# Transposing the hidden activations of the expert blocks on TensorE instead of VectorE

## The reference

```
def expert_block(args):                      # xb: rows of one expert, e: which one
    xb, e = args
    hb = jax.nn.silu(xb @ w_gate[e]) * (xb @ w_up[e])
    return hb @ w_down[e]

y = lax.map(expert_block, (buf.reshape(n_blocks, MOE_BLOCK, D), block_e)).reshape(n_blocks * MOE_BLOCK, D)
out = jnp.zeros((N, D), x.dtype).at[tok_sorted].add(y[dest] * w_sorted[:, None])
```

## Time and profile before

| | |
|---|---|
| median of 3 executions | 3587.28 us (3582.31 to 3591.69) |
| the profiled execution | 3582.31 us, its span 3580.3 us |
| mean granted TensorE clock in it | 0.934 of full speed |
| busy over the span | TensorE 3176.8 us (89%), VectorE 1404.8 (39%), ScalarE 673.8 (19%) |
| first expert stage | 408.31 to 714.46 us |
| second expert stage | 1163.58 to 1472.36 us |

### The profile page before, as it was taken

One profiled execution on the slowest core, in us unless ns is written; L12 is line 12 of the kernel. 1 busy time (PEld: TensorE's weight loads), 2 busy tenths in 40 slices (PEclk: granted clock), 3 DMA queues, 4 the chain that ended last, 5 costly groups with the idle time before them and its releaser, 6 DMA issues. The chain is left out here.

```text
span 3580.3 us, 42191 instructions
## 1 busy us (share of the span) xinstructions
PE 3176.8 (89%) x15899; PEld 1565.7 (44%) x15899; DVE 1404.8 (39%) x3366; ACT 673.8 (19%) x1430; POOL 341.1 (10%) x434
## 2 busy tenths in 40 slices
PE   8889698859967988479999999898699999999998
PEld 5455333324544333244444444664443443444344
DVE  6533333333352333408999920563322122212222
ACT  1143122132221222210110110452110101001011
POOL 0023011110202111100000000123000000000000
PEclk9999799969988999789999999999799999999999
DMA  7861799831013999443335345755399999999994
GB/s 261 230 251 66 260 372 366 307 110 45 12 60 111 356 364 361 176 171 113 121 119 130 115 147 177 299 194 206 116 396 406 422 406 405 404 423 406 405 410 203
DMA packets 282431, 886.16 MB, mean 248 GB/s; under 512 B 35704, under 2 KB 75520, under 8 KB 233168
## 3 DMA queue, kind: packets, MB, share of 16 engines
q1 hardware_dynamic: 254032, 806.79, 60.3%
q0 software_dynamic: 28288, 77.91, 6.1%
HBM read 803.59 MB, written 80.99 MB: 247 GB/s over the span
## 5 line engine op out<-in xcount | busy, mean ns | idle before, releaser
L3047 PE MATMUL ec_gu<-ec_ring,ec_xg 128*64 128x512 f32 x2048 | 454.6, 595 | 0.9 <-ACT ec_xg L3199 0.9
L245 PE MATMUL proj_ps<-xT,proj_w 128*128 128x512 f32 x992 | 431.9, 597 | 0.9 <-DMA proj_w<-in_na_w_in 0.9
L245 PE MATMUL proj_ps<-proj_w,xT 128*128 128x512 f32 (+2 forms) x896 | 358.4, 562 | 22.2 <-DMA proj_w<-in_w_in 22.2
L245 PEld LDWEIGHTS proj_ps<-xT,proj_w 128*128 128x128 f32 x992 | 189.7, 192 | 239.3 <-issue 237.7
L3047 PEld LDWEIGHTS ec_gu<-ec_ring,ec_xg 128*64 128x64 f32 x2048 | 142.0, 137 | 303.3 <-issue 303.3
L245 PEld LDWEIGHTS proj_ps<-proj_w,xT 128*128 128x128 f32 x896 | 171.4, 192 | 207.4 <-issue 154.6
L3076 PE MATMUL ec_yp<-ec_ring,ec_hT 128*64 128x512 f32 x1024 | 248.2, 635 | 0.0
L1350 PE MATMUL moe_gu_ps<-moe_w,moe_xg 128*64 128x512 f32 x1024 | 231.4, 605 | 17.6 <-DMA moe_w<-in_exp_w_up 11.3
L274 ACT ACTIVATE proj_o<-proj_ps 128x512 f32<-128x512 f32 (+1 forms) x120 | 70.8, 590 | 611.4 <-PE proj_ps L245 611.4
L1413 DVE TENSOR_TENSOR moe_sig<-moe_sig,moe_gu_ps 64x512 f32<-64x512 f32 x32 | 21.7, 679 | 395.3 <-ACT moe_up L1457 395.3
L2225 DVE SCALAR_TENSOR_TENSOR band_big<-proj_hit,proj_row,band_big 128x516 f32<-128x516 f32 x256 | 173.5, 751 | 2.4
(11 more groups left out here) (515 smaller groups left out, 3871.0 us busy)
## 6 DMA issues: line engine op xcount, KB each, us to landing
ec_ring<-in_w_gate SPq DMA_DIRECT2D x128, 1024.0 KB, 9.6
ec_ring<-in_w_up SPq DMA_DIRECT2D x128, 1024.0 KB, 11.7
ec_ring<-in_w_down SPq DMA_DIRECT2D x128, 1024.0 KB, 12.3
moe_w<-in_exp_w_gate SPq DMA_DIRECT2D x32, 2048.0 KB
moe_w<-in_exp_w_up SPq DMA_DIRECT2D x32, 2048.0 KB
moe_w<-in_exp_w_down SPq DMA_DIRECT2D x32, 2048.0 KB, 21.0
proj_w<-in_w_in SPq DMA_DIRECT2D x22, 2048.0 KB, 11.0
proj_w<-in_w_ada SPq DMA_DIRECT2D x16, 1536.0 KB
```

The costliest lines, as they stand in the source:

```text
L245: mm = nc.tensor.matmul(bank[0:jb["op"], 0:jb["ow"]], lhs, rhs, start=(k == 0), stop=(k == nk - 1))
L3047: mm = nc.tensor.matmul(gu_ps[n][half, :], xg[:, k, c0:c0 + CAP], w[:, m * D_FF + n * 512:m * D_FF + (n + 1) * 512], start=(k == 0), stop= ...
```

## The change

The hidden values are no longer turned by VectorE. After gate/up of both blocks TensorE multiplies each 64x128 piece of hid and thid with the identity (`turn_h`), into a PSUM bank h_ps, and VectorE copies the bank to hT with two instructions a block (`turn`). The bank is the second of the two that x had: x now has one bank for both halves (the very first half excepted, which uses h_ps before it is needed), so the second half of x is turned only after ScalarE has copied the first, and the order of the three engines is rewritten around that. hT_main and hT_tail become one counter, hT_ready, counted when a block's hT is complete.

```diff
-        x_ps = [st.ps(f"x_ps{h}") for h in range(2)]
+        x_ps, h_ps = st.ps("x_ps"), st.ps("h_ps")
...
                 def turn_x(b, r, i, h):
                     if h == 0:
                         pe.wait_ge(xs_ready[r], 16 * i + 16)
-                    pe.wait_ge(xg_copied, 2 * b + h - 1)
+                    pe.wait_ge(xg_copied, 2 * b + h + 1)
                     for c in range(4):
-                        mm = nc.tensor.transpose(x_ps[h][:, c * MB:(c + 1) * MB], xs[r][:, (4 * h + c) * P:(4 * h + c + 1) * P],
+                        mm = nc.tensor.transpose(x_ps[:, c * MB:(c + 1) * MB], xs[r][:, (4 * h + c) * P:(4 * h + c + 1) * P],
                                                  ident[0:MB, 0:MB])
                     mm.then_inc(turned, 1)
...
+                def turn_h(i, r):
+                    b = 2 * i + r
+                    pe.wait_ge(hid_main, b + 3)
+                    pe.wait_ge(hT_ready, b + 1)
+                    for f in range(KF):
+                        nc.tensor.matmul(h_ps[:, f * MAIN:(f + 1) * MAIN], hid[r][:, f * P:(f + 1) * P],
+                                         ident[0:MAIN, 0:MAIN], start=True, stop=True)
+                    pe.wait_ge(hid_tail, b + 3)
+                    for c in range(2):
+                        c0 = (KF + c) * MAIN
+                        mm = nc.tensor.matmul(h_ps[:, c0:c0 + MAIN], thid[r][:, c * P:(c + 1) * P], ident[0:MAIN, 0:MAIN],
+                                              start=True, stop=True)
+                    mm.then_inc(hT_ps_ready, 1)
+
                 def down(i, r):
                     b = 2 * i + r
-                    pe.wait_ge(hT_main, b + 1)
+                    pe.wait_ge(hT_ready, b + 2)
...
-                    pe.wait_ge(hT_tail, b + 1)
...
                 def body(i, more):
                     gate_up(i, 0)
                     turn_x(2 * i + 1, 1, i, 0)
+                    gate_up_tail(i, 0)
                     turn_x(2 * i + 1, 1, i, 1)
-                    gate_up_tail(i, 0)
                     gate_up(i, 1)
                     gate_up_tail(i, 1)
+                    turn_h(i, 0)
                     if more:
                         turn_x(2 * i + 2, 0, i, 0)
+                    down(i, 0)
+                    if more:
                         turn_x(2 * i + 2, 0, i, 1)
-                    down(i, 0)
+                    turn_h(i, 1)
                     down(i, 1)
...
-                    V.drain()
-                    for fq in range(P // QD):
-                        for tb in range(MAIN // QD):
-                            e = V.transpose(hT[r][fq * QD:(fq + 1) * QD, :, tb * QD:(tb + 1) * QD],
-                                            by_f(hid[r][tb * QD:(tb + 1) * QD, :])[:, :, fq * QD:(fq + 1) * QD])
-                    e.then_inc(hT_main, 1)
...
+                def turn(i, r):
+                    dve.wait_ge(hT_ps_ready, 2 * i + r + 1)
+                    V.tensor_copy(hT[r][:, :, 0:MAIN], h_ps[:, 0:KF * MAIN].rearrange("p (f s) -> p f s", s=MAIN))
+                    V.tensor_copy(hT[r][:, :, MAIN:MB].rearrange("p (h c) s -> p h c s", c=2),
+                                  h_ps[:, KF * MAIN:(KF + 2) * MAIN].rearrange("p (c h s) -> p h c s", c=2, h=2))
+                    V.drain().then_inc(hT_ready, 1)
+
                 def body(i):
                     hidden(i, 0)
                     hidden(i, 1)
+                    turn(i, 0)
+                    turn(i, 1)
...
                 def body(i, more):
                     main(i, 0)
                     copy_x(2 * i + 1, 1, 0)
+                    tail(i, 0)
                     copy_x(2 * i + 1, 1, 1)
-                    tail(i, 0)
                     main(i, 1)
                     tail(i, 1)
                     if more:
                         copy_x(2 * i + 2, 0, 0)
+                    rows_out(i, 0)
+                    if more:
                         copy_x(2 * i + 2, 0, 1)
-                    rows_out(i, 0)
                     rows_out(i, 1)
```

More of the change, by code:

```diff
@@ L1255, in moe_experts @@
     MB, MAIN, TAIL = MOE_ROWS, 64, 32
-    QD = 32
     lo, hi = slice(0, MAIN), slice(MAIN, P)
@@ L1275, in moe_experts @@
         hid_main, hid_tail = st.sem("hid_main"), st.sem("hid_tail")
-        hT_main, hT_tail = st.sem("hT_main"), st.sem("hT_tail")
+        hT_ps_ready, hT_ready = st.sem("hT_ps_ready"), st.sem("hT_ready")
         down_ready, y_copied = st.sem("down_ready"), st.sem("y_copied")
@@ L1324, in first_x @@
                 def first_x(h):
-                    bank = x_ps[h]
+                    bank = (x_ps, h_ps)[h]
                     for c in range(4):
@@ L1343, in gate_up @@
                     b = 2 * i + r
-                    pe.wait_ge(xg_copied, 2 * b + 2)
+                    pe.wait_ge(xg_copied, 2 * b + 3)
                     for n in range(2):
@@ L1406, in _ @@
                 dve.sem_inc(hid_tail, 2)
+                dve.sem_inc(hT_ready, 1)
                 n1 = pairs_less_one(dve)
-                by_f = lambda v: v.rearrange("p (f q) -> p f q", q=P)
                 def hidden(i, r):
@@ L1441, in _ @@
             def _(act):
+                act.sem_inc(xg_copied, 1)
                 act.sem_inc(turned, 1)
@@ L1447, in _, with copy_x @@
                 n1 = pairs_less_one(act)
-                def copy_x(b, r, h):
+                def copy_x(b, r, h, bank=x_ps):
                     act.wait_ge(turned, 2 * b + h + 2)
-                    nc.scalar.activation(xg[r][:, 4 * h:4 * h + 4, :].rearrange("p c s -> p (c s)"), x_ps[h][:, 0:4 * MB],
+                    nc.scalar.activation(xg[r][:, 4 * h:4 * h + 4, :].rearrange("p c s -> p (c s)"), bank[:, 0:4 * MB],
                                          ACT.Copy).then_inc(xg_copied, 1)
@@ L1480, in body @@
                         copy_x(2 * i + 2, 0, 0)
+                    rows_out(i, 0)
+                    if more:
                         copy_x(2 * i + 2, 0, 1)
-                    rows_out(i, 0)
                     rows_out(i, 1)
                 copy_x(0, 0, 0)
-                copy_x(0, 0, 1)
+                copy_x(0, 0, 1, h_ps)
                 with act.Fori(0, n1) as i:
```

## The result

The changed kernel takes 3623.02 us, the median of four executions (3619.35 to 3626.52), against 3589.14 for the kernel before, also four (3582.31 to 3591.69). The ratio is 1.0101, with a 95% interval of 1.0082 to 1.0121: the change costs about 1%. The forecast was 3618 in a range of 3598 to 3656. The execution profiled was the highest of its four, 3626.52 us (span 3624.6), and the one profiled before was the lowest of its four; the spans differ by 44.3 us, the medians by 33.9. Three more executions of the changed kernel are on record, at 3618.15, 3626.57 and 3634.03 us.

A forecast was written before the change was run, and what follows sets the result against it. DMA transfers were taken to set the expert stages' pace, TensorE having 3.1 to 3.9 us slack a pair. Layers added 18.3 + 14.6 = 32.9 us to the profiled 3582.31, giving 3615.2; forecast 3618, half way towards the median's base, range 3598 to 3656.

The forecast's parts named there:

- Wait A: Before gate/up of block 1: TensorE waits for ScalarE to copy x after block 0's tail; 1.1 us added a pair.
- Wait B: Before the first down: VectorE copies block 0's turned hidden values only after block 1's products; 1.9 us added a pair.
- Wait C: Between the two downs: turning block 1's hidden values, then waiting for VectorE's copies; 1.7 us added a pair.
- The chain: TensorE's path through one steady pair of blocks: 34.96 us without DMA wait, plus 4.7, makes 39.66 us.
- The turns: TensorE's 12 matmul records turning one block's hidden values: 0.12 us each, 1.4 us; rival at ec_h's 3.0 us, chance 0.12.
- The bound moves from DMA to TensorE: Steady pairs: 39.66 us on TensorE exceeds the transfers' 38.06 and 38.87, so only the part above the slack is paid.
- The rival "faster": Steady pairs: DMA waits come of queue order, so pairs follow TensorE's path; with 2 us added, 3575 us; chance 0.05.
- The clock: Rival at the downs: small work and waits drop TensorE to 1.2 GHz once a pair, 27 us, 3645; chance 0.16.
- the prediction's own sign: At the downs: the prediction is wrong if down rows show 5 us and more.
- The other signs: Steady pairs: 39.7 us, DMA share below 1, no moe_xs or w_up waits; about 0.9 and 1.1 us before the downs.
- First pairs: First pair of blocks in each expert stage: 3.6 us added in the first layer, 4.7 in the second.
- Last pairs: Last pair of blocks in each expert stage, without slack or x to turn: 1.1 + 2.7 + 1.3 = 5.1 us added.

The follow-up runs named there:

- the filler kernels: Kernel before the change, plus 3 or 6 pairs of unused full-width matmuls before each block pair's first down: 3602.99 us (ratio 1.0032) and 3623.04 us (1.0091).
- the kernel without the three waits: Changed kernel, reordered so x and hidden-value turns and copies leave no TensorE waits, down output's main rows copied early: 3590.79 us, ratio 0.9995.
- the kernel with the filler: Changed kernel plus two unused full-width matmuls on TensorE between turning block 1's hidden values and the second down: 3607.94 us, ratio 1.0036.
- the kernel with the transpose mode: Changed kernel with 4 of the 6 matmuls of each hidden-value turn issued as transposes: 3613.52 us, ratio 1.0051.
- the strided kernel: Changed kernel, but hidden-value turns load weights with a step of 4 elements (main) or 2 (tail) instead of contiguous: 3691.15 us, ratio 1.0267.

## Why the prediction was right, point by point

- *Wait A, +1.1 us.* From the tail's end to gate/up it took 1.55 us (507.94 to 509.49). Gate/up to the end of block 1's tail takes 23.25 us (496.85 to 520.10), 22.02 before: +1.23, so the term was 0.1 too low. Taking the wait away gave back 0.91.
- *Wait B, +1.9.* The down starts 2.46 us after the tail's slot (520.10 to 522.56), 0.80 before: +1.66, so the term was 0.2 too high. The terms written down in the prediction add to 2.56 and not 2.65; the copies were 0.41 and 0.27 us and overlap a little. VectorE's order is the chain that ends last, as named, but TensorE's turning ended only 0.2 us ahead of the copies, so another order on VectorE alone would have saved about that.
- *Wait C, +1.7.* 522.56 to 530.77 is 8.21 us, 6.69 before: +1.52.
- *The chain, 39.66 us.* Measured 39.37: the three terms add to 4.41 us instead of 4.7, A being a little larger, B and C smaller. B and C were priced as waits, though TensorE's own turning fills most of them.
- *The turns, 1.4 us a block, not ec_h's 3.0.* 1.48 from slot to slot, and the reason, the step of the weights, was shown by giving them that step.
- *The bound moves from DMA to TensorE, and only the part above the slack is paid.* Right: no DMA wait is left in the steady pairs, and the filler kernels give ratios of 1.003 and 1.009, 11 and 33 us, for 16 x 2.6 = 42 and 16 x 5.3 = 85 us of work. The rival "faster", by which a shorter chain would pay, falls with the kernel without the three waits: its chain of 37.15 is not followed, the six steady pairs take 38.1 us on average in the first layer and 38.3 in the second.
- *The clock* was a rival at 0.16, not in the sum, and it happened in part: 8 of 12 steady pairs, 8 x 1.7 = 13.6 us. It was left out of the sum, and it came. By the prediction's own sign (wrong if down rows show 5 us and more) it is wrong on this point, though the sign was ill chosen: five steady pairs of the kernel before had such rows already.
- *The other signs.* The DMA share was to fall below 1 and stood at 1.00 and 1.02; in the kernel with the filler it is 1.04 and no matmul waits for a transfer, so this share doesn't tell the two sides apart here. The waits before the downs were to be 0.9 and 1.1 us and were 0.43 and 0.74.
- *First pairs, +3.6 and +4.7.* They were +4.34 and +6.48. The rows of block 1 were turned 13.1 us into the stage (422.67 less 409.58) instead of 11.3, and the tail behind took 5.76 us instead of 3.66. *Last pairs, +5.1 each:* +4.73 and +4.58.

The sum for the profiled execution was 32.9 us. Term by term: chain and six pairs -3.5 (12 x 0.29), clock +13.6, first pairs +2.5, last pairs -0.9, which makes 44.6 against 44.3 measured between the spans. The sum was thus 11 us short, and the clock alone is more than that. The forecast of 3618 lies 5 us from the median, and that is in part luck: the profiled execution was the fastest before and the slowest of its four after, so the 44.3 us between the profiles are 33.9 between the medians, which happens to be close to a sum without the clock. Of the seven changed ones on record the one at 3634.03 us had a mean granted clock of 0.929 and the one at 3618.15 us 0.933, which would fit fewer slow downs in the faster ones; but there is only one trace of this kernel, so that is not shown.

Open stay two things. Why the slow downs start in one pair and not in the one ahead of it, with the same rows in front: the trace shows it and no reason. And the first pair of a stage, whose late rows were not varied by themselves.

## What to carry to other kernels

Ask of moved work not only what it costs on its new engine but also which waits its new order brings; here the work on TensorE, 3.3 us a pair, was about as long as the slack of 3.1 to 3.9 us, and 1.0 us more of waiting, with the clock, carried the chain over it. Read the slack of the engine that gets the work in the stage concerned, from the timeline with its DMA waits taken out, and charge only what exceeds it. A short stretch of small matmuls with a wait behind it can cost more through TensorE's clock than through the wait (1.70 us against 0.74 here), and a microsecond of unused full-width work in the wait can be a gain.

## What the runs showed of the hardware that was not expected

- A weight load of 128 float32 columns takes 188 ns contiguous, 193 with a step of 2 elements and 326 with a step of 4. A step of 2 is nearly free; it is not a matter of contiguous or not.
- The granted clock fell to the 1.2 GHz level in the second down after only 1.4 us of small matmuls and 0.74 us of idle, and not before the first down, where the wait is 0.43 us. In the kernel with the transpose mode it fell in the first down of five pairs, three times behind a wait of 1.07 or 1.08 us and twice behind a DMA wait ahead of x (1.86 and 0.75 us), and never in the second, whose wait is 0.74 us. With the slower turns of the strided kernel it fell for both in ten of twelve steady pairs. With 0.9 us of full-width matmuls in the wait it never fell in a steady pair, and neither did it in the kernel with 5.3 us of filler, whose 1.17 us wait stands behind a down's tail.
- The same transfers landed sooner in the changed kernel: w_down in 14.9 us instead of 20.8, the rows of x in 15.3 instead of 18.2, although a pair of the first layer is only 6% longer. The mean rate hardly moved (359 GB/s; 366 and 362 before).
